# A float32 block of ten stages: x loaded by column halves around the first weight slot, and the last tile's norm weights multiplied in ahead of its rstd

## The reference, cut to what matters

```python
def rms_norm(x, g):                        # every stage begins with it
    return x * rsqrt(mean(x * x, -1) + 1e-6) * g

def swiglu(h, w_gate, w_up, w_down):       # hidden width 2816, in chunks of 256
    return (silu(h @ w_gate) * (h @ w_up)) @ w_down

x = x + 0.5 * swiglu(rms_norm(x, g[0]), ffn_w_gate[0, 0], ffn_w_up[0, 0], ffn_w_down[0, 0])   # first stage
...
x = x + swiglu(rms_norm(x, norm_ffn), w_gate, w_up, w_down)                                    # last stage
return rms_norm(x, norm_final)
```

## Time and profile before

| what | value |
|---|---|
| median of 3 runs | 1309.23 us (1309.19 to 1309.44) |
| the profiled execution's own time | 1311.33 us |
| its span in the trace | 1309.6 us |
| TensorE busy | 1291.6 us, 99% of the span |
| VectorE, ScalarE, GpSimd busy | 847.0, 655.4, 82.1 us |
| granted TensorE clock, mean | 0.996 of full |
| moved by DMA | 256.87 MB, 196 GB/s in the mean |

### The profile page before, as it was taken

How to read it: one execution, slowest core, us unless ns; L and a number is a source line. 1 busy time by engine, 2 the same in 40 slices (tenths; PEclk the granted TensorE clock), 3 DMA queues, 4 the chain that set the end, 5 groups by cost and what they waited for, 6 DMA issues and landing times.

```text
span 1309.6 us, 17052 instructions
## 1 busy us (share of the span) xinstructions
PE 1291.6 (99%) x6249; PEld 1082.3 (83%) x6249; DVE 847.0 (65%) x929; ACT 655.4 (50%) x769; POOL 82.1 (6%) x195
## 2 busy tenths in 40 slices
PE   9999999999999999999999999999999999999997
PEld 7888889888888887888888877888888987888886
DVE  5655569876555567655556876555567887655554
ACT  6444457445444447544445855444447554544442
POOL 2000004100000002000001200000001200000000
PEclk9999999999999999999999989999999999999999
DMA  9766655446776645776663326666744551667772
GB/s 294 244 224 224 224 193 178 146 144 221 231 224 226 228 163 175 229 227 225 226 223 101 133 98 217 225 224 224 226 175 162 179 175 59 205 222 224 226 225 77
DMA packets 189563, 256.87 MB, mean 196 GB/s; under 512 B 9048, under 2 KB 151022, under 8 KB 189518
## 3 DMA queue, kind: packets, MB, share of 16 engines
q1 hardware_dynamic: 156560, 229.17, 53.1%
q10 hardware_dynamic: 32478, 26.30, 6.1%
q0 software_dynamic: 480, 0.80, 0.4%
HBM read 243.38 MB, written 12.85 MB: 196 GB/s over the span
## 4 chain that ended last, share of the span: by engine, by line
PE 93%; DVE 3%; ACT 2%; DMA 1%; issue 0%; SPq 0%; POOL 0%; DVEq 0%; POOLq 0%; ACTq 0%
PE ps L275 28%; PE ps L277 28%; PE ps L276 28%; PE ps L372 1%; DVE wl L247 1%; DMA raw<-in_ffn_w_up 1%; PE ps L302 1%; PE ps L303 1%; PE ps L304 1%; ACT wh L236 1%; PE ps L1242 1%; PE ps L666 0%; PE ps L281 0%; PE ps L2289 0%; PE ps L2295 0%
## 5 line engine op out<-in xcount | busy, mean ns | idle before, releaser
L275 PE MATMUL ps<-wl,hth 128*128 128x512 f32 (+3 forms) x1256 | 490.8, 391 | 3.0 <-DVE wl L247 1.6
L277 PE MATMUL ps<-wh,htl 128*128 128x512 f32 (+3 forms) x1256 | 485.0, 386 | 0.0
L276 PE MATMUL ps<-wh,hth 128*128 128x512 f32 (+3 forms) x1256 | 484.8, 386 | 0.0
L894 DVE TENSOR_TENSOR wl<-raw,wh 128x2048 fp32r<-128x2048 f32 x120 | 275.1, 2292 | 188.3 <-ACT wh L821 182.9
L821 ACT ACTIVATE wh<-raw 128x2048 fp32r<-128x2048 f32 x120 | 229.6, 1914 | 154.0 <-DMA bounce<-xn 91.0
L275 PEld LDWEIGHTS ps<-wl,hth 128*128 128x128 f32 x1256 | 236.4, 188 | 51.6 <-issue 5.0
L277 PEld LDWEIGHTS ps<-wh,htl 128*128 128x128 f32 x1256 | 236.3, 188 | 47.7
L276 PEld LDWEIGHTS ps<-wh,hth 128*128 128x128 f32 x1256 | 236.6, 188 | 45.3
L247 DVE TENSOR_TENSOR wl<-raw,wh 128x2048 fp32r<-128x2048 f32 (+3 forms) x94 | 207.7, 2215 | 68.7 <-ACT wh L236 67.9
L236 ACT ACTIVATE wh<-raw 128x2048 fp32r<-128x2048 f32 (+3 forms) x94 | 173.5, 1851 | 62.2 <-PE ps L277 42.2
L275 PE MATMUL ps<-wl,prod_h 128*128 128x512 f32 x400 | 156.1, 390 | 0.0
(11 more groups left out here) (423 smaller groups left out, 992.0 us busy)
## 6 DMA issues: line engine op xcount, KB each, us to landing
raw<-in_ffn_w_down SPq DMA_DIRECT2D x88, 512.0 KB, 4.0
raw<-in_ffn_w_gate SPq DMA_DIRECT2D x86, 512.0 KB, 4.2
raw<-in_ffn_w_up SPq DMA_DIRECT2D x86, 512.0 KB, 5.2
raw<-in_w_gate_up SPq DMA_DIRECT2D x44, 512.0 KB, 4.7
raw<-in_even_w_in SPq DMA_DIRECT2D x24, 512.0 KB, 4.6
bounce<-xn ACTq DMA_DIRECT2D x45, 256.0 KB, 2.9
xn<-bounce ACTq DMA_DIRECT2D x45, 256.0 KB, 4.9
raw<-in_w_down SPq DMA_DIRECT2D x22, 512.0 KB, 4.0
```

The lines of the kernel that those rows point to most:

```text
L275: nc.tensor.matmul(o, xh, b, start=first, stop=False)
L276: nc.tensor.matmul(o, xh, a, start=False, stop=False)
L277: return nc.tensor.matmul(o, xl, a, start=False, stop=last)
L894: nc.vector.tensor_tensor(wl[:, r, :], raw[:, r, :], wh[:, r, :].bitcast(f32), ALU.subtract)\
```

## The change

At the start, x is loaded as two column halves (features 0 to 511 ahead of slot 0, features 512 to 1023 between slots 0 and 1), each two requests of 256 KB. TensorE turns banks 0 and 1 only, does all 24 matmuls of slot 0, and turns banks 2 and 3 behind them; the other parameter rows are turned behind slot 1. ScalarE and VectorE take banks and half slots in turn: bank 0, slot 0a, bank 1, slot 0b, bank 2, slot 1a, bank 3, slot 1b. Ten of the eleven parameter requests are issued by GpSimd, and ScalarE makes a one-column copy first, so that its function table is loaded before the gain columns are there. The transposes of the identity are 16 in place of 24.

At the end, the left half of tile 1 is multiplied by the gain row ahead of its rstd and scaled by ScalarE afterwards; VectorE instead of GpSimd adds the two partial sums of tile 1; tile 0 is normed in two halves, of which the second and its store lie behind that sum; the left half's store waits for ScalarE.

```diff
 
+        def split_high_part(act, n, j):
+            loaded, done = ((first_loaded[n], first_high), (raw_loaded[n], high_ready))[j]
+            act.wait_ge(loaded, 32)
+            nc.scalar.activation(first_part(wh, n, j), first_part(raw, n, j), ACT.Copy).then_inc(done, 1)
+
+        def split_low_part(dve, n, j):
+            ready, done = ((first_high, first_low), (high_ready, split_ready))[j]
+            dve.wait_ge(ready, n + 1)
+            nc.vector.tensor_tensor(first_part(wl, n, j), first_part(raw, n, j), first_part(wh, n, j).bitcast(f32),
+                                    ALU.subtract).then_inc(done, 1)
...
         def norm_act(act, s, gain, banks=(0, 1, 2, 3)):
             if s == 0:
                 turn_act(act, s, 0, KT, gain, banks, part=(0, 1))
-                act_ahead.through(act, 0)
-                turn_act(act, s, 0, KT, gain, banks, part=(1, 3))
-                act_ahead.through(act, 1)
+                split_high_part(act, 0, 0)
+                turn_act(act, s, 0, KT, gain, banks, part=(1, 2))
+                split_high_part(act, 0, 1)
+                turn_act(act, s, 0, KT, gain, banks, part=(2, 3))
+                split_high_part(act, 1, 0)
                 turn_act(act, s, 0, KT, gain, banks, part=(3, 4))
+                split_high_part(act, 1, 1)
+                act_ahead.n = 2
             elif PLAN[s] == "hybrid":
                 for u in range(2):
                     half_tile_act(act, s, 1, u, gain)
...
 
 
 
+        def load_x(sp, half):
+            for tt in range(TT):
+                o = slice(half * 512, half * 512 + 512)
+                sp.dma_start(x[:, tt, o], io["x"][0, tt * P:(tt + 1) * P, o]).then_inc(x_loaded[half], 16)
+
         def ffn_load(sp, n, w_gate, w_up, w_down):
             g = w_gate.rearrange("(k p) n -> p k n", p=P)
             u = w_up.rearrange("(k p) n -> p k n", p=P)
...
+                        load_x(sp, 1)
                 else:
                     load_slot(sp, n + j, gate_up(n + j, j, 0))
...
                     turn_x(pe, s, 0, FFN_BANKS[0])
                     turn_x(pe, s, 1, FFN_BANKS[1])
                 if s == 0:
+                    for b in range(2):
+                        w = [slice(kk * 2 * HC, (kk + 1) * 2 * HC) for kk in (2 * b, 2 * b + 1)]
+                        ks = (2 * b, 2 * b + 1)
+                        high_by(pe, s, 0, b + 1)
+                        if b == 0:
+                            pe.wait_ge(first_high, 1)
+                        else:
+                            pe.wait_ge(high_ready, 1)
+                        for k in ks:
+                            for tt in range(TT):
+                                nc.tensor.matmul(bank(tt), hth[:, k, tt * P:(tt + 1) * P], wh[:, 0, w[k % 2]], start=k == 0, stop=False)
+                        turned_by(pe, s, 0, b + 1)
+                        for k in ks:
+                            for tt in range(TT):
+                                nc.tensor.matmul(bank(tt), htl[:, k, tt * P:(tt + 1) * P], wh[:, 0, w[k % 2]], start=False, stop=False)
+                        if b == 0:
+                            pe.wait_ge(first_low, 1)
+                        else:
+                            take_slot(pe, 0)
+                        for k in ks:
+                            for tt in range(TT):
+                                m = nc.tensor.matmul(bank(tt), hth[:, k, tt * P:(tt + 1) * P], wl[:, 0, w[k % 2]], start=False, stop=False)
+                    m.then_inc(weights_used, 1)
                     turn_x(pe, s, 2, FFN_BANKS[2])
                     turn_x(pe, s, 3, FFN_BANKS[3])
-                if s == 0:
-                    high_by(pe, s, 0, 1)
-                    pe.wait_ge(first_high, 1)
-                    w = [slice(kk * 2 * HC, (kk + 1) * 2 * HC) for kk in range(2)]
-                    for k in range(2):
-                        for tt in range(TT):
-                            nc.tensor.matmul(bank(tt), hth[:, k, tt * P:(tt + 1) * P], wh[:, 0, w[k]], start=k == 0, stop=False)
-                    turned_by(pe, s, 0, 1)
-                    for k in range(2):
-                        for tt in range(TT):
-                            nc.tensor.matmul(bank(tt), htl[:, k, tt * P:(tt + 1) * P], wh[:, 0, w[k]], start=False, stop=False)
-                    pe.wait_ge(first_low, 1)
-                    for k in range(2):
-                        for tt in range(TT):
-                            nc.tensor.matmul(bank(tt), hth[:, k, tt * P:(tt + 1) * P], wl[:, 0, w[k]], start=False, stop=False)
-                    turn_other_rows()
                 for b in range(4):
-                    if s == 0 and b == 0:
+                    if s == 0 and b < 2:
                         continue
                     if s == 0 and b == 2:
                         pe.wait_ge(first_low, b // 2 + 1)
                     turned_by(pe, s, 0, b + 1)
                     for k in (2 * b, 2 * b + 1):
                         gate_up(n + b // 2, k)
-                    if b == 0 and s > 0:
+                    if b == 0:
                         turn_x(pe, s, 2, FFN_BANKS[2])
                         turn_x(pe, s, 3, FFN_BANKS[3])
+                if s == 0:
+                    turn_other_rows()
 
             def first_by_tiles(pe):
 
...
 
             def normed(tt, o, rstd_of):
                 dve.wait_ge(FIN_POOL.sem, FIN_POOL.after(rstd_of))
-                nc.vector.scalar_tensor_tensor(out=xn[:, tt, o], in0=x[:, tt, o], scalar=rstd[:, tt:tt + 1],
-                                               in1=gain_row[:, o], op0=ALU.mult, op1=ALU.mult).then_inc(rows_ready, 1)
+                return nc.vector.scalar_tensor_tensor(out=xn[:, tt, o], in0=x[:, tt, o], scalar=rstd[:, tt:tt + 1],
+                                                      in1=gain_row[:, o], op0=ALU.mult, op1=ALU.mult)
 
             dve.wait_ge(final_ready, 1)
             FIN_DVE.done(nc.vector.tensor_tensor(x[:, 0, :], x[:, 0, :], ps[:, 4:6, :], ALU.add), "sum0")
             dve.wait_ge(final_ready, 2)
             FIN_DVE.done(nc.vector.tensor_tensor(x[:, 1, 0:HD], x[:, 1, 0:HD], bank(6), ALU.add), "sum1a")
+            dve.wait_ge(gain_loaded, 16 * (PLAN.count("ple") + 1))
+            dve.wait_ge(FIN_DVE.sem, FIN_DVE.after("sum1a"))
+            FIN_DVE.done(nc.vector.tensor_tensor(xn[:, 1, 0:HD], x[:, 1, 0:HD], gain_row[:, 0:HD], ALU.mult), "gained1a")
             dve.wait_ge(weights_used, n)
             FIN_DVE.done(nc.vector.tensor_tensor(x[:, 1, HD:D], x[:, 1, HD:D], bank(7), ALU.add), "sum1b")
-            dve.wait_ge(FIN_DVE.sem, FIN_DVE.after("sum1b"))
-            dve.wait_ge(gain_loaded, 16 * (PLAN.count("ple") + 1))
-            normed(0, slice(0, D), "rstd0")
-            normed(1, slice(0, HD), "rstd1")
-            normed(1, slice(HD, D), "rstd1")
+            normed(0, slice(0, HD), "rstd0")
+            dve.wait_ge(FIN_POOL.sem, FIN_POOL.after("eps1"))
+            dve.wait_ge(FIN_ACT.sem, FIN_ACT.after("square1b"))
+            FIN_DVE.done(nc.vector.tensor_tensor(mean_sq[:, 1:2], mean_sq[:, 1:2], last_sq, ALU.add), "total1")
+            normed(0, slice(HD, D), "rstd0").then_inc(rows_ready, 1)
+            normed(1, slice(HD, D), "rstd1").then_inc(rows_ready, 1)
 
         def final_act(act):
             for tt, o, at, name in ((0, slice(0, D), mean_sq[:, 0:1], "0"), (1, slice(0, HD), mean_sq[:, 1:2], "1a"),
...
                 act.wait_ge(FIN_DVE.sem, FIN_DVE.after("sum" + name))
                 FIN_ACT.done(nc.scalar.activation(final_sq[:, tt, o], x[:, tt, o], ACT.Square, scale=1 / math.sqrt(D), accum_out=at),
                              "square" + name)
+            act.wait_ge(FIN_POOL.sem, FIN_POOL.after("rstd1"))
+            FIN_ACT.done(nc.scalar.activation(xn[:, 1, 0:HD], xn[:, 1, 0:HD], ACT.Copy, scale=rstd[:, 1:2]), "normed1a")
 
         def final_pool(pool):
-            for tt, name in ((0, "0"), (1, "1a")):
-                v = mean_sq[:, tt:tt + 1]
-                pool.wait_ge(FIN_ACT.sem, FIN_ACT.after("square" + name))
-                pool_link(pool, nc.gpsimd.tensor_scalar(v, v, EPS, None, ALU.add))
-                if tt == 1:
-                    pool.wait_ge(FIN_ACT.sem, FIN_ACT.after("square1b"))
-                    pool_link(pool, nc.gpsimd.tensor_tensor(v, v, last_sq, ALU.add))
-                FIN_POOL.done(nc.gpsimd.tensor_tensor(rstd[:, tt:tt + 1], v, minus_half[:, 0:1], ALU.pow), f"rstd{tt}")
+            v = mean_sq[:, 0:1]
+            pool.wait_ge(FIN_ACT.sem, FIN_ACT.after("square0"))
+            pool_link(pool, nc.gpsimd.tensor_scalar(v, v, EPS, None, ALU.add))
+            FIN_POOL.done(nc.gpsimd.tensor_tensor(rstd[:, 0:1], v, minus_half[:, 0:1], ALU.pow), "rstd0")
+            v = mean_sq[:, 1:2]
+            pool.wait_ge(FIN_ACT.sem, FIN_ACT.after("square1a"))
+            FIN_POOL.done(nc.gpsimd.tensor_scalar(v, v, EPS, None, ALU.add), "eps1")
+            pool.wait_ge(FIN_DVE.sem, FIN_DVE.after("total1"))
```

(22 more changed lines are left out.)

39 lines of the change are left out of this document (17 added, 22 removed).

## The result

| | before | changed |
|---|---|---|
| median of the runs | 1309.28 us (1309.19 to 1309.69, 6 runs) | 1313.80 us (1313.10 to 1315.52, 6 runs) |
| ratio to before | | 1.0034, 95% interval 1.0024 to 1.0044 |
| profiled execution, own time / span | 1311.33 / 1309.6 us | 1313.78 / 1312.0 us |

The change makes the kernel slower by 4.5 us (0.34%; the interval is 3.1 to 5.8 us). That lies inside the range given (1308.6 to 1313.9), but 2.6 above the predicted time, and on the side that had a chance of 0.29, not 0.68. It is inside by 0.1 us and by luck: the upper bound was set for a clock that falls in the new gap, and in the profiled execution, which lies at the median, it did not fall there.

The account below looks back on a forecast made before the run. TensorE, busy 99% of the span, was taken to bound the kernel, so only its two ends could move: +2.1 us at the start and -0.1 at the end make +2.0, from 1309.2 to 1311.2 us, range 1308.6 to 1313.9.

Parts of the forecast that it names:

- The clock in the new gap: Rival: the clock falls while TensorE idles 2.6 us ahead of slot 1, costing +2.2 us, to 1313.4; chance 0.25.
- Step 1: Loads at the start: x's first half there at about 4.65 us, with no price for x's smaller requests.
- Step 2: TensorE's beginning: 16 transposes end by 5.0, first matmul at 7.35 us instead of 8.97, 1.6 us earlier.
- Step 3: Slot 0 done in one piece at the start: its 24 matmuls take 5.5 us, to 12.85.
- Step 4: Bank 2 turned only behind slot 0, at 13.35; ScalarE waits there, slot 1a's copy begins at 14.1, 2.45 us later.
- Steps 5 and 6: Slots 1 and 2: slot 2's copy at 18.8; TensorE waits 2.6 us for slot 1a, slot 2 at 23.05, 2.3 later.
- Step 7: Slot 3's chain: product ready at about 28.2, before TensorE by 0.3; turned at 28.5 instead of 26.42, +2.1 us.
- The end: Last sum to last store: about 1 us won on the engines, nearly all lost to the stores' queue, -0.1 us.
- The offset between execution and median: Whole run: the median was taken as 2.1 us below the profiled execution, so 1313.3 became 1311.2.
- An even start: Rival: slot 3's landing at 19.1 still sets the product's turn at 26.42, giving 1309.1, or 1308.1; chance 0.12.
- The low stretch near 756: Rival: the low-clock stretch around 756 us gets shorter; half its 3.0 us gives 1309.7, all 1308.2; chance 0.18.

Follow-up runs that it names:

- e5: The kernel before with only x changed, loaded in four requests of half rows, left halves of both tiles first: 1310.85 us, one execution.
- e3: The changed kernel with the old end, so the changed start alone: 1313.81 us, ratio 1.0036 to the kernel before.
- e6: e3 with GpSimd's ten parameter requests held until x's first half has landed: 1312.74 us, one execution.
- e11: e3 with x loaded whole, in two requests of 512 KB ahead of slot 0: 1316.61 us, one execution.
- e4: e3 with TensorE turning banks 2 and 3 of x between slot 0's halves instead of behind them: 1310.89 us, ratio 1.0009 to the kernel before.
- e7: e3 with slot 1's splits ahead of banks 2 and 3 in ScalarE's and VectorE's queues: 1311.83 us, ratio 1.0016 to the kernel before.
- e1: The kernel before run again with no edit, for a second trace: ratio 1.0001, median 1309.81 us.
- e8: The kernel before with another end, GpSimd doing only the power for tile 1, four stores of 256 KB: 1309.33 us, ratio 0.9997.

## Why the prediction was right and wrong

- **Step 1, loads: wrong, and the term that was mis-sized.** I gave the smaller requests no price, from a window of 356 GB/s in which requests of 256 KB were queued. x's first half landed at 1.25 + 4.29 = 5.54, not 4.65; the rate of all loads at 3 to 5 us is 222 and 254 GB/s where it was 416 and 405, and e5 shows that the split slows x. The queued requests of the earlier trace rows were parts of weights at 5 to 10 us, another place and another shape. But the windows of the changed kernel hold parts of slot 0 too, so the comparison of like with like is e5's: 296 and 304. And on this kernel's path the term is worth little: TensorE waited 0.18 us for x, in e3's trace and e6's not at all on the chain to the first matmul. The Trainium skill's rule against small requests (DMA: Bandwidth & Descriptors, Measured (HBM→SBUF, 128 partitions, SWDGE, issued from GpSimd)) pointed the right way; its reading as one request after the other, 4 us, was too large against the 0.9 us on x's first half here and the 1.8 us on all of x in e5.
- **Step 2: mis-sized by itself.** First matmul at 8.43, not 7.35. The 16 transposes of the identity took 3.68 us, not 2.9 to 3.4, and with the gain rows TensorE was done at 5.39, not at 5.0; then 0.18 us for x; then its first four transposes of x took 0.83 and not 0.5. ScalarE began bank 0 at 6.50 (5.45), and the rest followed. I had taken the mean of 24 transposes for the first 16, but the first ones are the slow ones: in the kernel before, the window from 3 to 4 us holds 7 matmuls and that from 5 to 6 us 11. In e3 and e11, with 16, all eight first transposes of x are slow too (421 ns in the median); in the five traces with 24 the median is 272 or 273. No run changes the 16 alone.
- **Step 3: right.** 5.57 us for slot 0 (5.5).
- **Step 4, the deciding one: right.** Banks 2 and 3 at 14.00, directly behind slot 0; ScalarE idle until TensorE releases it. e4 gives 2.9 us back by moving eight transposes, e7 2.0 from the other side.
- **Steps 5 and 6: right in their differences.** From slot 1a's copy to slot 2's 4.69 us (4.7); TensorE's wait 2.70 (2.6); slot 2 on TensorE 1.3 later than given (24.36, not 23.05), all but 0.2 of it from the first matmul.
- **Step 7: right.** The product was there at 28.64 + 0.88 = 29.52, ahead of TensorE at 29.94. In all the start cost +3.5 (against the earlier trace rows) or +3.7 (against e1), not +2.1; of the 1.4 missing 1.1 is step 2, of which 0.2 from step 1. With the end's +0.2 the traces account for 3.7 to 3.9 of the 4.5 us between the medians; the clock falling in the gap in some executions could be the rest, which is not shown.
- **The end: -0.1 forecast, +0.2 in the trace** (6.90 against 6.70 in the traced execution of before and 6.74 in e1). Tile 0's store was 0.46 later behind the last square (0.4). The power began 1.23 us behind the square (1.13), but took 1.00, not 0.57, so the last two stores came at 3.01 and 3.40 us behind it where I had 2.4 and 2.5, and the stores went through in 2.85 us, not 2.5 (by the prediction's own numbers it is 2.96 less the gap of 0.3, 2.7). I had carried 0.57 over from a place where VectorE was idle; the earlier trace rows had the sign, an addition of one column that took 0.51 us beside VectorE's norm.
- **The offset between execution and median: wrong.** I took 2.1 us off, because the traced execution of before lay that far above its median. That belonged to this one execution with its long low stretch near 756 us (e1's is 0.4 above). The changed kernel's lies on its median. Of the 2.6 us by which 1311.2 missed, 0.5 is the difference of the profiled executions (1313.3 forecast, 1313.78 measured: 1.7 too little at both ends, 1.2 too much for what lies between, where the low stretch was half as long) and 2.1 this offset.
- **The rivals.** The clock in the new gap is real, but not in each execution: not in the changed kernel's trace nor in e6, in e3 and e11 yes. An even start did not come. The low stretch near 756 was shorter in the changed kernel's trace: 3.4 us (the row below is its first window, and that from 762 to 764 us is at 0.57 too), as long as in e1 and half of what the earlier trace rows come from. It is absent in e3, e5, e6, e8 and e11. It varies from execution to execution, in the kernel before too, so it is not shown to hang on the change; what it does to the difference of the medians no trace can say.

```profile
760.00:762.00 2.00, 2.00 (x7) 0.57 0.69 197
```

## What to carry to other kernels

When a piece of work is moved later in one engine's order, look at what stands behind its consumer in the consumer's queue: here eight transposes, 1 us in all, placed 2.7 us later, held a queue whose next entry had its data (slot 1a, there by 11.7). A load that is split so that its first half comes sooner has to be priced at the rate of its new shape at that moment, not at the rate of full queues later, and then laid beside what the engine that waits for it is still busy with. The first operations of an engine are priced by their own rows, not by a mean that takes in the later ones. And when the sum is made against one profiled execution, know first how far that execution is from others of the same kernel.
